# Cross attention with half-size products for keys and queries, and a first projection on rows without the root

## The chip, the core and the metric

The kernel runs on one core of a Trainium2 chip. TensorE multiplies, VectorE (DVE) and ScalarE (ACT) add, scale, copy and take functions, GpSimd (POOL) helps a little, and SyncE (SP) issues the weight transfers. The metric is the time of one execution on the device in microseconds; of several runs the median counts.

## The reference, cut to what matters

Two transformer blocks follow each other over 256 tokens of width 1024, in float32. The first block has two layers. Each layer is a mixer (a gated recurrence with forgetting attention in layer 0, dilated and sliding-window attention in layer 1), then cross attention to 256 memory rows, then an MLP with squared relu. The second block is a hybrid mixer and a mixture of 16 experts. The change touches the first projection of layer 0 and the cross attention of both layers:

```python
def rmsnorm(x, g):
    y = x * rsqrt(mean(x * x, axis=-1) + EPS)
    return y * g
z = rmsnorm(h, ab_norm) @ w_in        # u, gate, q, k, v, f_logit are its parts
...
mem_n = rmsnorm(mem, g_mem)
q = (h @ w_q).reshape(b, s, 4, 256)   # h is rmsnorm(h, xa_norm) here
k, v = split(mem_n @ w_kv, 2)
sc = einsum("bqhd,bkhd->bhqk", q, k) * 256 ** -0.5
o = einsum("bhqk,bkhd->bqhd", softmax(sc), v)
out = o.reshape(b, s, 1024) @ w_o
```

## The kernel before, in words

Activations lie transposed: 128 partitions hold one chunk of the width, the free dimension holds the 256 tokens, and a tile such as `xT` or `hT` has eight chunks. Dense weights come in units of 1024 rows by 512 columns (2 MB) through a ring of six slots. SP issues unit after unit in a fixed order; a unit for a slot waits until the products that read the slot's former unit are done (`unit_read`, L1436). The order of work on each engine is written out by hand; engines meet at semaphores. `filled` and `freed` count uses of the eight PSUM banks; `full` waits for a finished bank, `copied` for one that has been read out.

`columns` multiplies one unit: for each of four groups of 128 output columns eight products accumulate (weights stationary 128x128, rows moving, 256 columns), 32 in all. The profile shows each such float32 product as two MATMUL records with two weight loads. `mm` (L482) is the helper that most of them share.

At the start SP loads x and waits for it before it issues unit 0. TensorE runs 24 fillers on a constant tile (L825). ScalarE squares x, TensorE sums the squares over the partitions with a tile of ones (`norm("ab")`, eight products), ScalarE takes the root, VectorE the reciprocal (L1919), and scales the rows by root and gain into `hT` (L1927). Then TensorE makes `ab_f` (eight columns of forget logits), `ab_u` (unit 0), `ab_gate` (unit 1), the gates' small products and the units for q, k and v. ScalarE copies `ab_u` into the padded tile `up`, on which VectorE runs the convolution. Ahead of that VectorE computes a short chain of decay constants (`log1p` on `sp_t`, up to L2045).

Cross attention of a layer (`cross`) is two key units (`columns` on the memory rows `raw`, banks 5 and 6 for the first), the product of the norm's sum between them, two value units, two query units, the attention of four heads of 256, and the output projection. The value units (L885) already use seven products of half-size blocks in place of eight (a Winograd form of Strassen's scheme): VectorE forms four sums of weight blocks (`vw`, 128x1024 each) and four of memory-row blocks (`vh`, 128x512 each) in `prepare_values`, and combines the products in `collect_values` (L2158 and on). There the rows are stationary and 256 weight columns move. The up-projection of the MLP (`up_columns`, L941) uses the same scheme the other way round: weight blocks are stationary, 128 tokens move, 56 products for a unit. ScalarE copies keys and queries out of PSUM, the queries with the factor 1/16. Scores of heads 0 and 1 come between the halves of the second query unit. VectorE first normalizes `hT` for the queries (`norm`), then prepares the value sums.

Further on, from some 1180 us, the expert weights (96 units of 2 MB) stream in.

## Time and profile before

| | us |
|---|---|
| median of 3 runs (1681.64 to 1685.13) | 1684.67 |
| the profiled execution's own time | 1685.47 |
| its span, first to last instruction | 1683.7 |
| TensorE busy | 1502.4 (89%) |
| VectorE busy | 693.7 (41%) |
| ScalarE busy | 288.8 (17%) |
| mean granted TensorE clock, as a share | 0.944 |

The span is what the rows cover. A busy TensorE is the sum of stretches in which a matmul record was open. In rows of a timeline the second number is the length of the group, and a bracket gives the engine's idle time before it and what released it. In rows of groups the mean is that of one record.

### The profile page before, as it was taken

The numbers are of one execution on the slowest core, as the hardware profiler recorded it, in microseconds if no ns is written. First come the engines' busy times: TensorE is split into PE (matmuls) and PEld (weight loads), VectorE is DVE, ScalarE is ACT, GpSimd is POOL, SyncE is SP. The second block draws the span as 40 slices with busy tenths as digits, with TensorE's granted clock in tenths as the row PEclk, the third lists the DMA queues.
The fourth block names the chain that finished last, engine by engine and source line by source line (L and its number), as shares of the span: only waits on it lengthen the run. The fifth ranks groups of instructions, "written<-read, shape, count | busy, mean of one in ns | idle before, by whom it ended". The sixth has DMA issues, their size and how long they took to land.

```text
span 1683.7 us, 22615 instructions
## 1 busy us (share of the span) xinstructions
PE 1502.4 (89%) x9686; PEld 1157.3 (69%) x9686; DVE 693.7 (41%) x1448; ACT 288.8 (17%) x722; POOL 30.2 (2%) x52
## 2 busy tenths in 40 slices
PE   9999999999999999999999999989988566665666
PEld 7878889998877788899988887768863221221211
DVE  4635218788524441288876746823230000000000
ACT  1332012310112411222101322221020000000000
POOL 0000000000010000000000111000000000000000
PEclk9999999999999999999999999988999897888777
DMA  9525415866433053257763003232889999999997
GB/s 382 199 86 194 156 51 213 306 267 227 176 118 144 20 193 144 80 223 305 270 229 138 1 11 115 101 101 101 349 334 427 428 428 428 428 429 428 429 429 330
DMA packets 45107, 396.44 MB, mean 235 GB/s; under 512 B 16208, under 2 KB 18640, under 8 KB 20176
## 3 DMA queue, kind: packets, MB, share of 16 engines
q1 hardware_dynamic: 44304, 393.51, 58.7%
q8 instruction: 77, 1.26, 0.3%
q0 software_dynamic: 272, 1.05, 0.2%
q10 hardware_dynamic: 432, 0.44, 0.1%
q14 instruction: 22, 0.18, 0.0%
HBM read 392.36 MB, written 2.63 MB: 235 GB/s over the span
## 4 chain that ended last, share of the span: by engine, by line
PE 75%; DMA 22%; DVE 1%; SPq 1%; ACT 1%; issue 1%; DVEq 0%; ACTq 0%
PE pb L482 41%; DMA ring<-in_w_experts 21%; PE pb L977 11%; PE pb L941 10%; PE pb L580 7%; PE pb L885 3%; DMA inverses_turned<-arena 1%; PE pb L649 1%; SPq L1440 0%; PE pb L825 0%; ACT arena L1503 0%; PE pb L707 0%; SPq L1397 0%; ACT hT L1503 0%; PE pb L988 0%
## 5 line engine op out<-in xcount | busy, mean ns | idle before, releaser
L482 PE MATMUL pb<-hT,ring 128*128 128x256 f32 x1216 | 278.0, 387 | 0.0
L482 PEld LDWEIGHTS pb<-hT,ring 128*128 128x128 f32 x1216 | 232.5, 193 | 39.3 <-issue 7.8
L482 PE MATMUL pb<-ring,hT 128*32 128x512 f32 (+2 forms) x896 | 145.8, 656 | 62.9 <-DMA ring<-in_w_experts 61.7
L482 PEld LDWEIGHTS pb<-ring,hT 128*32 128x32 f32 (+1 forms) x896 | 45.1, 131 | 153.1 <-DMA ring<-in_w_experts 82.3
L1503 ACT ACTIVATE arena<-pb 128x512 f32<-128x512 f32 (+4 forms) x141 | 65.2, 477 | 366.8 <-PE pb L482 272.1
L2703 DVE SCALAR_TENSOR_TENSOR side<-side,pb 128x256 f32<-128x256 f32 x16 | 6.7, 421 | 272.2 <-ACT side L1503 272.2
L580 PE MATMUL pb<-arena,ring 128*128 128x256 f32 x512 | 118.6, 383 | 0.0
L580 PEld LDWEIGHTS pb<-arena,ring 128*128 128x128 f32 x512 | 95.3, 191 | 14.7 <-issue 2.9
L1503 ACT ACTIVATE side<-pb 128x256 f32<-128x256 f32 (+2 forms) x44 | 18.5, 421 | 442.5 <-PE pb L482 424.7
L482 PE MATMUL pb<-arena 128*64 128x128 f32 (+4 forms) x464 | 71.2, 338 | 4.6 <-DVE sml L1978 2.7
L482 PE MATMUL pb<-arena,hT 128*32 128x512 f32 x216 | 38.8, 845 | 35.5 <-DMA arena<-in_w_experts 23.2
L482 PEld LDWEIGHTS pb<-arena 128*64 128x64 f32 (+2 forms) x464 | 50.6, 173 | 23.3 <-issue 18.8
L2177 DVE CUSTOM_DVE_ANT_0 ring<-ring,arena,cols 128x1024 f32<-128x1024 f32 x48 | 59.2, 1281 | 0.0
L977 PE MATMUL pb<-ring,arena 128*128 128x256 f32 x256 | 58.2, 379 | 0.0
L977 PE MATMUL pb<-arena,hT 128*128 128x256 f32 x256 | 57.9, 379 | 0.0
L977 PE MATMUL pb<-ring,hT 128*128 128x256 f32 x256 | 57.9, 379 | 0.0
L482 PE MATMUL pb<-arena,side 128*32 128x256 f32 (+1 forms) x464 | 43.3, 474 | 15.6 <-DMA arena<-in_w_experts 8.9
L482 PE MATMUL pb<-root_pairs,ring 128*128 128x256 f32 (+1 forms) x288 | 54.3, 338 | 0.7 <-DMA ring<-inverses 0.7
L941 PE MATMUL pb<-hT,ring 128*128 128x128 f32 x448 | 54.6, 275 | 0.0
L2715 DVE TENSOR_TENSOR arena<-pb,rstd 128x256 f32<-128x256 f32 x16 | 6.8, 425 | 113.6 <-PE pb L482 113.6
L977 PEld LDWEIGHTS pb<-arena,hT 128*128 128x128 f32 x256 | 48.6, 190 | 6.6
L977 PEld LDWEIGHTS pb<-ring,hT 128*128 128x128 f32 x256 | 48.6, 190 | 6.6
(376 smaller groups left out, 2187.2 us busy)
## 6 DMA issues: line engine op xcount, KB each, us to landing
ring<-in_w_dense SPq DMA_DIRECT2D x86, 2048.0 KB, 8.0
ring<-in_w_experts SPq DMA_DIRECT2D x63, 2048.0 KB, 41.0
arena<-in_w_experts SPq DMA_DIRECT2D x22, 2048.0 KB, 40.7
arena<-in_w_experts SPq DMA_DIRECT2D x10, 1024.0 KB, 36.8
cons<-in_w_experts SPq DMA_DIRECT2D x10, 1024.0 KB, 40.1
ring<-in_w_dense SPq DMA_DIRECT2D x2, 1536.0 KB, 7.1
ring<-in_w_experts SPq DMA_DIRECT2D x4, 512.0 KB, 36.1
cons<-in_cons SPq DMA_DIRECT2D x1, 1808.0 KB, 17.9
```

Of the source, the lines that this page charges most:

```text
L482: return nc.tensor.matmul(o, l, r, start=st, stop=sp)
L580: last = nc.tensor.matmul(proj["banks"][c // 2][:, (c % 2) * S:(c % 2 + 1) * S], w[:, k, (c % 4) * P:(c % 4 + 1) * P], yT[:, k, :], start= ...
L649: last = nc.tensor.transpose(ps[:, c:c + P], pr2[:, n % 4, qb, kb * P:(kb + 1) * P], ident)
L885: last = nc.tensor.matmul(pv[j[0]][:, FEAT[j[1]]], rows_[l](k), cols_[r](k), start=k == 0 and n < 4, stop=k == 3, skip_group_check=True)
L941: last = nc.tensor.matmul(ps[b][:, o:o + P], lhs[x][:, k, f * P:(f + 1) * P], rhs[x][:, k, :], start=x in "156" and f == 0 and k == 0, sto ...
L977: last = nc.tensor.matmul(pq[j[0]][:, FEAT[j[1]]], rows_[l](k), cols_[r](k), start=g == 0 and k == 0 and n < 4, stop=g == 3 and k == 3, sk ...
L1503: return nc.scalar.activation(o, i, f, **kw)
L2177: ins = V.tensor_tensor_reduce(out=w, in0=w, in1=c_row, scale=1.0, scalar=col("b_ada", 4 * i + f), op0=ALU.mult, op1=ALU.add, accum_out=mo ...
L2703: V.scalar_tensor_tensor(tg[:, e % 2, :], tg[:, e % 2, :], 1.0, ps[:, 0:S], ALU.add, ALU.mult).then_inc(eg_ready, 1)
L2715: V.tensor_tensor(yq[:, e % 2, :], ps[:, 0:S], rs[:, :], ALU.mult).then_inc(free, 1)
```

## The change

At the start the wait for x on SP goes, and unit 0 comes in four quarters, each with a semaphore. VectorE scales the rows of x by the gain only (`raw_x`), sums the squares in pairs as other norms do, and TensorE multiplies unit 0 with these rows right behind 20 fillers (`first_unit`), one chunk of the width after the other, with one product of the squares' sum after the third chunk. VectorE multiplies `ab_u` by the reciprocal root when it copies it into `up`; ScalarE does not copy it any more. `ab_f` comes behind `ab_u`.

In cross attention the second key unit and both query units go through `cross_columns`: seven products of half-size blocks, each eight matmuls of 128 moving tokens with stationary weight blocks, in the order 1, 5, 6, 7, 4, 2, 3. The weight sums go through the three buffers `vw` (the fourth is formed in place in the slot), the row sums through `vh`: those of the memory rows serve the keys and then the values, those of `hT` both query units. ScalarE copies the first product (`first_block`) and the last block (`last_block`); VectorE adds the other three blocks (`block_22`, `block_21`, `block_12`). The factor 1/16 moves into the gain of the norm (`g16`). Value units keep their products; their weight sums are now single steps (`weight_sum`) between others. The scaling of the memory rows for layer 1 moves behind the norm's pair sums.

```diff
-        SUMMED = ("mem", "xa0", "mlp0", "cd", "xa1", "mlp1", "final")
+        SUMMED = ("ab", "mem", "xa0", "mlp0", "cd", "xa1", "mlp1", "final")
...
+            def first_unit():
+                u = at[0]
+                at[0] += 1
+                w = slot_ap(u)
+                ps = [fill(f"ab_u{b}") for b in range(2)]
+                for k in range(DC):
+                    if k % 2 == 0:
+                        if k < 6:
+                            pe.wait_ge(first_part[k // 2], 16)
+                        else:
+                            pe.wait_ge(loaded[slot_of[u]], 16)
+                    pe.wait_ge(raw_x_ready, k + 1)
+                    for b in range(2):
+                        for j in range(2):
+                            last = nc.tensor.matmul(ps[b][:, j * S:(j + 1) * S], w[:, k, (2 * b + j) * P:(2 * b + j + 1) * P], raw_x[:, k, :],
+                                                    start=k == 0 and j == 0, stop=k == DC - 1, skip_group_check=True)
+                        if k == DC - 1:
+                            mark(last, f"ab_u{b}", u=u if b else None)
+                    if k == 2:
+                        norm_of_sum("ab")
...
-            for i in range(24):
+            for i in range(20):
...
-            norm("ab")
+            first_unit()
...
-            columns("ab_u", hT)
...
+            def cross_columns(layer, which, banks, middle=None):
...
+                place = {"1": (0, 0), "2": (0, 0), "4": (0, 1), "5": (1, 0), "3": (1, 0), "6": (2, 0), "7": (2, 1)}
+                lhs = {"1": w[:, HALF[0], FEAT[0]], "5": vw[0], "6": vw[1], "7": w[:, HALF[0], FEAT[1]], "4": vw[2],
+                       "2": w[:, HALF[1], FEAT[0]], "3": w[:, HALF[1], FEAT[1]]}
+                rhs = {"1": m[0][:, :, TOK[0]], "5": vh[0], "6": vh[1], "7": vh[2], "4": m[1][:, :, TOK[1]],
+                       "2": m[1][:, :, TOK[0]], "3": vh[3]}
+                for x in "1567423":
+                    b, side_ = place[x]
+                    name = f"x{which}{layer}_{b}"
+                    if x in "156":
+                        ps[b] = fill(name, banks[b])
+                    if x in "5674":
+                        pe.wait_ge(vw_ready, weight_sums(layer, which, "5674".index(x) + 1))
+                    if which != "q1" and x in "5673":
+                        pe.wait_ge(vh_ready, 8 * layer + 4 * (which == "q0") + "5673".index(x) + 1)
+                    if x == "4":
+                        pe.wait_ge(q1_copied, n + 1)
+                    if x == "3":
+                        pe.wait_ge(out_ready, blocks_out_of(layer, which, 1))
+                    for f in range(2):
+                        for k in range(4):
+                            if which == "q0" and x == "1" and f == 0:
+                                pe.wait_ge(h_ready, (8, 32)[layer] + k + 1)
+                            o = side_ * S + f * P
+                            last = nc.tensor.matmul(ps[b][:, o:o + P], lhs[x][:, k, f * P:(f + 1) * P], rhs[x][:, k, :],
+                                                    start=x in "156" and f == 0 and k == 0, stop=x not in "15" and k == 3,
+                                                    skip_group_check=True)
+                    mark(last, name, True, u if x == "3" else None)
+                    product_done["cross", layer, which, x] = (banks[b], marks[banks[b]])
+                    if x == "6" and middle is not None:
+                        middle()
...
-                columns(f"xk{layer}_1_", raw)
+                cross_columns(layer, "k", (4, 7, 5))
...
+                cross_columns(layer, "q0", (0, 1, 2))
...
+                cross_columns(layer, "q1", (3, 6, 7), first_scores)
...
-            sp.wait_ge(x_in, 16)
...
+                if u == 0:
+                    for i in range(4):
+                        part = slice(i * UNIT // 4, (i + 1) * UNIT // 4)
+                        sp.dma_start(t[:, at:at + UNIT][:, part], w[:, part]).then_inc(first_part[i] if i < 3 else loaded[slot_of[u]], 16)
+                elif u < len(units) - 1:
...
-            act.wait_ge(pads, 1)
-            for i in range(2):
-                copy(f"ab_u{i}", up[:, 2 * i:2 * i + 2, 3:3 + S], pairs)
...
+            def first_block(layer, which):
+                b, m = product_done["cross", layer, which, "1"]
+                act.wait_ge(filled[b], m)
+                fn(block_of(layer, which)[1], pairs(pb[:, b, :])[:, 0, :].rearrange("p (f t) -> p f t", f=2), ACT.Copy).then_inc(q1_copied, 1)
+            def last_block(layer, which):
+                b, _, use = fillings[f"x{which}{layer}_0"]
+                act.wait_ge(out_ready, blocks_out_of(layer, which, 2))
+                fn(block_of(layer, which)[0], pairs(pb[:, b, :])[:, 0, :].rearrange("p (f t) -> p f t", f=2), ACT.Copy).then_inc(freed[b], 1)
...
-                for j in range(2):
-                    copy(f"xk{layer}_1_{j}", kT[:, 4 + 2 * j:6 + 2 * j, :], pairs)
+                first_block(layer, "k")
+                last_block(layer, "k")
...
-                for i in range(3):
-                    copy_q(i)
-                attention(f"xa{layer}", None, lambda: copy_q(3))
+                first_block(layer, "q0")
+                last_block(layer, "q0")
+                first_block(layer, "q1")
+                attention(f"xa{layer}", None, lambda: last_block(layer, "q1"))
...
+            dve.wait_ge(x_in, 16)
+            for c in range(DC):
+                V.tensor_scalar(raw_x[:, c, :], xT[:, c, :], col("ab_norm", c), None, ALU.mult).then_inc(raw_x_ready, 1)
+            sum_pairs("ab")
+            V.tensor_scalar(g16, cols[:, COLS["xa_norm0"][0]:COLS["xa_norm0"][0] + 16], 1.0 / 16, None, ALU.mult).then_inc(g16_ready, 1)
...
+            for i in range(2):
+                ps, free = full(dve, f"ab_u{i}")
+                dve.wait_ge(pads, 1)
+                V.tensor_tensor(up[:, 2 * i:2 * i + 2, 3:3 + S], pairs(ps), by_rstd(2), ALU.mult).then_inc(free, 1)
...
-            dve.wait_ge(mn_ready, 8)
-            V.tensor_tensor(memT, memT, by_rstd(DC), ALU.mult).then_inc(mn_ready, 1)
...
+                dve.wait_ge(g16_ready, 1)
+                dve.wait_ge(mn_ready, 9 * layer + 8)
+                for x in (1, 2, 3):
+                    row_sum(layer, "k", x)
+                    weight_sum(layer, "k", x)
                 sum_pairs(f"xa{layer}")
-                norm(f"xa{layer}", lambda c: col(f"xa_norm{layer}", c))
-                prepare_values(layer, 0)
-                prepare_values(layer, 1)
+                weight_sum(layer, "k", 4)
+                row_sum(layer, "k", 4)
+                if layer == 0:
+                    V.tensor_tensor(memT, memT, by_rstd(DC), ALU.mult).then_inc(mn_ready, 1)
+                weight_sum(layer, "v0", 1)
+                weight_sum(layer, "v0", 2)
+                block_22(layer, "k")
+                block_21(layer, "k")
+                weight_sum(layer, "v0", 4)
+                weight_sum(layer, "v0", 3)
+                block_12(layer, "k")
+                norm(f"xa{layer}", lambda c: g16[:, 8 * layer + c:8 * layer + c + 1])
+                for x in (1, 2, 4, 3):
+                    weight_sum(layer, "v1", x)
                 collect_values(layer, 0)
+                dve.wait_ge(h_ready, (16, 40)[layer])
+                for x in (1, 2):
+                    row_sum(layer, "q0", x)
+                    weight_sum(layer, "q0", x)
+                weight_sum(layer, "q0", 3)
+                weight_sum(layer, "q0", 4)
+                row_sum(layer, "q0", 3)
+                row_sum(layer, "q0", 4)
                 collect_values(layer, 1)
-                attention(f"xa{layer}")
+                weight_sum(layer, "q1", 1)
+                weight_sum(layer, "q1", 2)
+                block_22(layer, "q0")
+                weight_sum(layer, "q1", 3)
+                block_21(layer, "q0")
+                weight_sum(layer, "q1", 4)
+                block_12(layer, "q0")
+                def last_queries(h):
+                    if h == 0:
+                        block_22(layer, "q1")
+                        block_21(layer, "q1")
+                        block_12(layer, "q1")
+                attention(f"xa{layer}", last_queries)
...
-                m = [view(t, 0, 4, S) for t in (lru_w_, rtp)]
+                if n == 1:
+                    dve.wait_ge(loaded[slot_of[u]], 16 * nth[u])
...
+                    ins = V.tensor_tensor(vw[0], w12, w11, ALU.subtract)
+                elif n == 2:
+                    ins = V.tensor_tensor(vw[1], w22, vw[0], ALU.subtract)
+                elif n == 3:
+                    ins = V.tensor_tensor(w12, w22, w12, ALU.subtract)
+                else:
+                    ins = V.tensor_tensor(vw[2], vw[1], w21, ALU.subtract)
+                ins.then_inc(vw_ready, 1)
...
+            def product_of(b, side_):
+                return pb[:, b, FEAT[side_]].rearrange("p (f t) -> p f t", f=2)
+            def block_22(layer, which):
+                c11, c12, c21, c22 = block_of(layer, which)
+                dve.wait_ge(q1_copied, 3 * layer + THREE.index(which) + 1)
+                b = after_product(layer, which, "7")
+                link(V.tensor_tensor(c12, c12, product_of(b, 0), ALU.add))
+                V.tensor_tensor(c21, c12, product_of(b, 1), ALU.add).then_inc(freed[b], 1)
+                copied(dve, f"x{which}{layer}_2")
+                b = after_product(layer, which, "5")
+                V.tensor_tensor(c22, c21, product_of(b, 0), ALU.add).then_inc(out_ready, 1)
+            def block_21(layer, which):
+                dve.wait_ge(out_ready, blocks_out_of(layer, which, 1))
+                after_product(layer, which, "2")
+                b = after_product(layer, which, "4")
+                c21 = block_of(layer, which)[2]
+                V.tensor_tensor(c21, c21, product_of(b, 1), ALU.subtract).then_inc(out_ready, 1)
+            def block_12(layer, which):
+                b = after_product(layer, which, "3")
+                c12 = block_of(layer, which)[1]
+                V.tensor_tensor(c12, c12, product_of(b, 0), ALU.add).then_inc(freed[b], 1)
```

## Rows read from the trace of the kernel before

**Rows 1.** The page's chain that ended last, shares by engine.

```profile
PE 75%; DMA 22%; DVE 1%; SPq 1%; ACT 1%; issue 1%; DVEq 0%; ACTq 0%
```

**Rows 2.** Stretches: us, busy time by engine, clock, DMA share, GB/s.

```profile
1170.00:1180.00 10.00, 10.00 (x54) 7.93 (x53) 4.83 (x8) 0.00 (x0) 0.00 (x0) 1.00 0.01 2
1180.00:1190.00 10.00, 10.00 (x49) 8.79 (x48) 3.44 (x5) 0.00 (x0) 0.00 (x0) 1.00 0.87 339
1300.00:1400.00 100.00, 60.07 (x534) 21.22 (x529) 5.08 (x12) 5.73 (x17) 0.00 (x0) 0.88 1.01 429
```

**Rows 3.** What the DMA-issuing queue waited for: total us, times, longest.

```profile
SPq L1436 <- PE pb L482: 841.5, 106, 95.7
```

**Rows 4.** Timeline of the start: start us, us, engine, line, what, [idle, releaser].

```profile
1.05 7.37 PE L825 MATMUL pb<-more 128*128 128x128 f32 x48 [1.05 <-DVE more L2027]
...
6.38 2.56 ACT L1503 ACTIVATE arena<-xT 128x256 f32<-128x256 f32 x8 [2.54 <-DMA xT<-in_xT]
6.74 0.17 DVE L2029 TENSOR_SCALAR sml<-cols 128x4 f32<-128x4 f32 x1 [5.74 <-DMA cols<-in_cols]
...
8.27 3.62 PE L482 MATMUL pb<-arena,cons 128*128 128x256 f32 x16
...
12.49 1.75 DVE L1919 RECIPROCAL rstd<-root 128x256 f32<-128x256 f32 x1 [5.16 <-ACT root L1503]
...
14.28 3.26 DVE L1927 SCALAR_TENSOR_TENSOR hT<-xT,cols,rstd 128x256 f32<-128x256 f32 x8
...
14.91 5.30 PE L482 MATMUL pb<-hT,small_w 128*8 128x256 f32 x16 [3.03 <-DVE hT L1927]
...
20.14 27.89 PE L482 MATMUL pb<-hT,ring 128*128 128x256 f32 x128
...
20.92 0.47 DVE L2045 TENSOR_SCALAR arena<-pb,cols 8x256 f32<-8x256 f32 x1
...
54.95 1.14 DVE L2072 TENSOR_SCALAR side<-side,sml 128x256 f32<-128x256 f32 x4
```

**Rows 5.** A stretch of the start, columns as in rows 2.

```profile
15.00:17.00 2.00, 2.00 (x6) 0.60 (x6) 2.00 (x6) 0.00 (x0) 0.00 (x0) 0.50 1.05 451
```

**Rows 6.** DMA issues until 60 us: KB each, us to landing.

```profile
xT<-in_xT SPq DMA_DIRECT2D x1, 1024.0 KB, 5.6
...
cols<-in_cols ACTq DMA_DIRECT2D x1, 140.0 KB, 5.5
```

**Rows 7.** Timeline of TensorE in cross attention and MLP of layer 0.

```profile
148.42 1.89 PE L482 MATMUL pb<-lru_w,ring 128*128 128x256 f32 x8
...
162.24 1.89 PE L885 MATMUL pb<-ring,lru_w 128*128 128x256 f32 x8
...
272.33 1.95 PE L941 MATMUL pb<-hT,ring 128*128 128x128 f32 x16
...
284.84 1.95 PE L941 MATMUL pb<-hT,ring 128*128 128x128 f32 x16
```

**Rows 8.** Timeline of VectorE in cross attention of layer 0.

```profile
138.79 2.29 DVE L2098 TENSOR_TENSOR side<-side,rstd 128x2048 f32<-128x2048 f32 x1
140.99 2.14 DVE L1951 TENSOR_TENSOR arena<-arena 128x512 f32<-128x512 f32 x3
...
154.15 1.22 DVE L2130 TENSOR_TENSOR arena<-ring 128x1024 f32<-128x1024 f32 x1
155.28 0.69 DVE L2132 TENSOR_TENSOR arena<-lru_w,root_pairs 128x512 f32<-128x512 f32 x1
...
174.62 0.42 DVE L2158 TENSOR_TENSOR arena<-arena,pb 128x256 f32<-128x256 f32 x1 [1.12 <-PE pb L885]
```

**Rows 9.** Timeline of TensorE at two waits of cross attention.

```profile
217.49 0.60 PE L707 MATMUL pb<-cons,arena 128*128 128x128 f32 x4
218.70 1.53 PE L482 MATMUL pb<-arena 128*128 128x256 f32 x6 [0.61 <-ACT arena L1503]
...
616.29 1.97 PE L885 MATMUL pb<-ring,lru_w 128*128 128x256 f32 x8 [0.78 <-ACT arena L1503]
```

More of the change, by code:

```diff
@@ L865, in cross @@
                     value_unit[layer, i] = u
-                    n_ = 2 * layer + i
                     pv = {}
@@ new lines, in after_product, with weight_sum @@
+            def after_product(layer, which, x):
+                if which[0] == "v":
+                    b, done = product_done["value", layer, int(which[1]), (0, 4, 6, 1, 2, 3, 5)["1432567".index(x)]]
+                else:
+                    b, done = product_done["cross", layer, which, x]
+                dve.wait_ge(filled[b], done)
+                return b
+            def weight_sum(layer, which, n):
+                u = value_unit[layer, int(which[1])] if which[0] == "v" else cross_unit[layer, which]
+                order = (1, 2, 4, 3) if which[0] == "v" else (1, 2, 3, 4)
```

92 lines of the change are left out of this document (49 added, 43 removed).

## The prediction

> **What bounds the kernel now.** I read four views. First the chain that ended last: TensorE holds 75% of the span, the DMA engines 22% [rows 1]. Second, where the one gives way to the other. From 1170 to 1180 us TensorE is busy all the time and the DMA engines 1% of it; in the next ten microseconds they are busy 87%, and in the expert stage (1300 to 1400) 101% at 429 GB/s, while TensorE waits for weights [rows 2]. So the kernel has a part bound by TensorE, up to about 1180 us, and a part bound by the stream of expert weights behind it. Third, what starts that stream: the queue that issues the weights spent 841.5 us waiting for products at L482 alone, 106 times, to free a ring slot [rows 3]. The stream is of fixed length and hangs on TensorE's progress, so a microsecond cut from TensorE before 1180 us should come off the end too. Fourth, the places of the change: the first 48 us, and cross attention in both layers. In the reader's rows TensorE idles 3.03 us near the start [rows 4] and 0.61 and 0.78 us in cross attention [rows 9]; otherwise it goes from one product to the next. What is removed from TensorE there is a gain, if VectorE and ScalarE keep up.
>
> **The start, step by step.** Now the order on TensorE is: 24 fillers (1.05 to 8.4), eight products of the square sums (from 8.27), root, reciprocal (12.49, 1.75), eight scalings (14.28, 3.26), then `ab_f` at 14.91, `ab_u` at 20.14 [rows 4]. `ab_u` and `ab_gate` together are 128 records in 27.89 us; a product of 256 columns is two records, so one product costs 0.436 us and a unit of 32 costs 13.9 us; `ab_gate` begins at 20.14 + 13.95 = 34.1 us. The stretch from 15 to 17 us, right behind the idle time, shows 0.50, the lower of the two levels, 1.2 GHz, which is why `ab_f` takes 5.2 us where eight products at 0.436 would be 3.5 [rows 4, 5].
>
> After the change TensorE multiplies unit 0 by rows that carry only the gain; the root moves to VectorE's copy of the result. When can it begin? Twenty fillers instead of 24 save four at the later, faster pace: a pass of 128 columns is 0.112 us (12.51 / 112) [rows 7], two each, 0.9 us, so they end near 7.5. x is there at 6.38 and the columns of constants at 6.74 [rows 4]; four scalings of this shape take 1.14 us [rows 4], so raw row 0 is ready at about 7.1 and all eight at 9.1. The first quarter of the weights, 512 KB, sits right behind x in the queue: at the stream's 429 GB/s [rows 2] it needs 1.2 us, so it lands near 7.8 and each following one 1.2 us later, while TensorE wants one per 3.5 us. Start: 7.8. The unit takes 13.9, the one product of the summed squares 0.4 inside it, `ab_f` 3.5 at the full clock, since no idle stretch is left ahead of it. `ab_gate` begins at 25.6 instead of 34.1: **8.5 us less**.
>
> What must stay hidden for that. The square sum: squares done 6.38 + 2.56 = 8.94; three pair sums 2.14 (as the same three at 140.99 [rows 8]) and a last one of 0.42 end at 11.9; TensorE asks for it after the third row chunk, 7.8 + 12 x 0.436 = 13.0. Then root, reciprocal and eight scalings, 0.5 + 1.75 + 3.26, end at 19.2 and `ab_f` asks at 22.1. VectorE then does the small chain of the decay constants, 3.4 us in all (now between the end of the scalings at 17.5 and the next operation at 20.92 [rows 4]), to 22.6, and the two copies with the reciprocal root, 0.7 us each as any 512-wide operation [rows 8], to 24.0. `ab_gate` needs their banks at 25.6. Smallest slack here 1.1 us. Without that cover each microsecond late is one lost. The convolution behind it starts earlier than now, so nothing in the recurrence is later against TensorE. On SP the wait for x goes; all later issues wait for products and move with them. The fillers' end is the other side: were x there sooner, 7.5 is the floor; that is 0.3 more.
>
> **Cross attention, step by step.** The second key unit runs from 148.42 (its first product) to 162.24 (first value product): 13.82 us for 32 products of 256 columns [rows 7]. The new form is 7 x 8 = 56 products of 128 columns. The up-projection of the MLP already has that form (L941, seven products per unit, stationary weights, the same shapes): one unit from 272.33 to 284.84, 12.51 us [rows 7]. So a unit saves 1.31 us, and three units in each of two layers **7.9 us**.
>
> At this place the Trainium skill has a rule that speaks against the change (TensorE: Matmul & The Clock Gate, Back-to-back issue gap): with a weight load ahead of each product it measures about 81 ns per product at 128 columns against 56 alone. By it the half-size products would lose 45%: 12.51 x 81 / 56 = 18.1 us per unit, 4.3 more than now, and the kernel would be 26 us slower in these units by that estimate. The rows have the very pairing, at 112 ns per record of 128 columns where half of a 256-column record is 108; so the loads cost 4%, not 45%, and I go by the rows.
>
> Now the sums. VectorE gets per unit four weight sums of 1.22 us, for keys and first queries four row sums of 0.69 (those of the keys only move ahead, the values used them already), and five block sums of 0.42; ScalarE's four 512-wide copies per pair of units become two 256-wide ones per unit of some 0.3 us (2.56 / 8) [rows 4]. Per layer new on VectorE: 12 x 1.22 + 4 x 0.69 + 15 x 0.42 = 23.7 us in some 80 us of TensorE's time. I followed the order in layer 0, in times of the old trace. Keys: three row and three weight sums, 5.7 us at most, now stand before the pair sums of the norm, and the scaling of the memory rows, 2.29 us, moves behind them. From 138.8 that makes 138.8 + 5.7 + 2.1 + 0.4 = 147.0 [rows 8]; TensorE asks for the sum one product ahead of 148.42, at 148.0: slack 1.0, the smallest. The fourth sums end at 148.9, wanted at 155.5. The seventh product is done at 155.6 and the block sums 1.4 us later; the last product asks at 159.1. Values: their first sum is ready at 153, wanted at 164. Queries: the row buffers are free when the second value unit has used them, 178.2, 179.9, 183.4, 185.1; the sums end at 186.0; the first query unit starts at 185.1 and wants them one by one from 186.9 to 195.8. The second wants its sums from 199.4, has them from 190 to 197.8. Its block sums stand behind two row maxima and one scaling, are done at 210.3 in this frame, wanted at 211.8. So all of it lies beside TensorE, each with a microsecond or more left.
>
> Two waits change. At the end of the queries TensorE resumes 1.21 us after the turn's start (217.49 to 218.70), because a 512-wide copy stood ahead [rows 9]. Afterwards the last thing is one block sum: it starts 0.3 us behind the last product's end as at 174.62 [rows 8], takes 0.42, so about 0.8: 0.4 less, twice, **0.8 us**. In layer 1 the value unit waited 0.78 us for a bank that ScalarE had yet to copy (616.29) [rows 9]; the new keys use other banks, and that wait goes, with its restart **0.9 us**. Bounds: nothing to 1.7 together.
>
> **Sum.** 8.5 + 7.9 + 0.8 + 0.9 = 18.1 us. The profiled execution took 1685.5 us around a span of 1683.7; that gives 1667.4. The median of the runs shown is 1684.67, 0.8 below the profiled one, which gives 1666.6. I say 1667.0.
>
> **Rivals.** (a) The start brings less, because x and the gains come later once the queue is full. x needed 5.6 us and the small constants, on another queue, 5.5 [rows 6], with little beside them; now 2 MB of unit 0 and then more stand behind x at once. If the quarters share the engines with both, x comes up to 2 MB / 429 GB/s = 4.9 us later, the gain is 3.6 instead of 8.5: 1672. For it: the two queues already ran side by side. Against it: unit 0 is issued after x on the same queue. The Trainium skill says that descriptors of one queue start in order on each DMA engine but that transfers issued by different engines interleave (DMA: Bandwidth & Descriptors, Two DMAs through the same engine are not ordered, Issuing engines are not separate DMA queues); by that x keeps its place and only the constants can slip. No row of before settles it. If TensorE waits so long that the clock falls again, some 2 us more go.
>
> (b) The gain is hidden: TensorE is shorter, but the expert stream ends when it did. This needs a stream that does not follow TensorE; DMA share 0.01 just before it and the waits for products [rows 2, 3] speak against. 1685.
>
> (c) Slower: VectorE becomes the bound of the cross units. Place: each product waits for a sum that waits for the buffer of the product before. If none of it were covered, a unit would pay 4 x 1.22 + 3 x 0.42 and its row sums, about 7 us, six units 42: 1667 + 42 = 1709. It decides from 3 us uncovered per unit (18.1 / 6). For it: only three weight buffers and long chains of waits; against it: the slacks above, and the up-projection, which runs the same scheme with no idle time ahead of its products between 272 and 285.
>
> (d) The change doesn't do what it says, for instance the 56 products run slower from these tiles: half the unit gain, 1671, in the range of the first.
>
> **How the numbers follow.** Forecast 0.80 (own range 1664.5 to 1670, from the floor of 7.5, the two waits at their bounds, and one microsecond each way for where low-clock stretches fall); (a) and (d) 0.13; (b) 0.03; (c) 0.04. The 80% range takes in (a): 1664 to 1673. No change that a measurement could tell is within 0.2%, 3.4 us: faster 0.93, same 0.03, slower 0.04.
>
> **What would show it.** In the trace of after: first products of the ring's weights at about 7.8 us and the clock at 1.00 from then on; `ab_gate` at 25.6; seven groups of 16 records at 1.79 us in each cross unit; no idle of TensorE over 0.5 us from the keys to the scores; the stream's onset 18 us earlier, at 1163. A late x, an idle stretch ahead of "3" products, or an onset that stays at 1181 would prove it wrong.

## The result, and the profile after

The changed kernel took 1660.54 us, median of 4 runs (1657.76 to 1667.34), beside 1684.90 of the kernel before: ratio 0.9865, 95% interval 0.9831 to 0.9899. The forecast was 1667.0 with a range of 1664 to 1673; the kernel is faster than the range allows. The profiled execution took 1657.76 us around a span of 1656.0, 27.7 less than before, where the sum promised 18.1.

A few words are used throughout. A landmark is the start of one and the same product in two traces. The onset is the issue of the first transfer of expert weights on SP's queue. The work of a change is what it takes from TensorE's time between landmarks that have no stretch at the lower clock between them. Only at the start does it count a stretch at the lower clock with it: the 1.7 us that `ab_f` lost behind the idle time, which the change removes.

The page's chain of waits, by engine, which answers to [rows 1], and behind it the weight queue's largest group of waits, against [rows 3] (the new form of the cross units, at L926, has another 80.7 us of them).

```profile
PE 74%; DMA 23%; DVE 1%; SPq 1%; ACT 1%; issue 0%; DVEq 0%; ACTq 0%
```

```profile
SPq L1513 <- PE pb L498: 725.8, 99, 90.8
```

Stretches of the changed kernel, columns as in [rows 2]. The full-rate stream of expert weights, which began behind 1180 us before, now begins at 1150.70; in the expert stage the stream runs at the same rate (428 GB/s, 429 before).

```profile
1140.00:1150.00 10.00, 10.00 (x55) 7.92 (x54) 4.67 (x7) 0.00 (x0) 0.00 (x0) 1.00 0.01 2
1150.00:1160.00 10.00, 10.00 (x48) 8.81 (x47) 3.44 (x5) 0.00 (x0) 0.00 (x0) 1.00 0.91 357
1300.00:1400.00 100.00, 61.63 (x520) 21.18 (x512) 5.07 (x12) 5.70 (x17) 0.00 (x0) 0.84 1.01 428
```

The timeline of the start, against [rows 4]; behind it the stretch of [rows 5] and the two DMA issues of [rows 6].

```profile
8.39 2.19 DVE L2115 TENSOR_SCALAR arena<-xT,cols 128x256 f32<-128x256 f32 x8 [7.39 <-DMA cols<-in_cols]
8.89 5.42 PE L854 MATMUL pb<-arena,ring 128*128 128x256 f32 x24 [1.48 <-DVE arena L2115]
12.67 0.42 DVE L2036 TENSOR_TENSOR arena<-arena 128x256 f32<-128x256 f32 x1
14.15 0.59 PE L498 MATMUL pb<-arena,cons 128*128 128x256 f32 x2
17.14 3.26 DVE L2011 SCALAR_TENSOR_TENSOR hT<-xT,cols,rstd 128x256 f32<-128x256 f32 x8
23.30 3.62 PE L498 MATMUL pb<-hT,small_w 128*8 128x256 f32 x16
26.85 14.08 PE L498 MATMUL pb<-hT,ring 128*128 128x256 f32 x64
40.77 3.62 PE L498 MATMUL pb<-side,lru_w 128*128 128x256 f32 x16
```

```profile
15.00:17.00 2.00, 2.00 (x11) 1.76 (x10) 1.65 (x1) 1.90 (x4) 0.00 (x0) 1.00 0.88 371
```

```profile
xT<-in_xT SPq DMA_DIRECT2D x1, 1024.0 KB, 5.8
cols<-in_cols ACTq DMA_DIRECT2D x1, 140.0 KB, 7.1
```

The first of the four quarters of the weights, and below it the recurrence's small products in the kernel before:

```profile
ring<-in_w_dense SPq DMA_DIRECT2D x1, 512.0 KB, 7.0
```

```profile
47.87 3.62 PE L482 MATMUL pb<-side,lru_w 128*128 128x256 f32 x16
```

`ab_f` now runs at 1.00, in 3.62 us instead of 5.30, and `ab_gate` stands at 26.85. The first product came at 8.89 because VectorE had to wait for the columns of constants, which now need 7.1 us from issue to landing where they needed 5.5 [rows 6]. The first quarter, issued at 1.23 us, was there at about 8.2. The recurrence's small products (L498, `side` x `lru_w`) were at 47.87 before and are at 40.77: the start gives 7.1 us.

TensorE in the second key unit of layer 0, against [rows 7], and at the end of the queries, against [rows 9]:

```profile
141.32 1.95 PE L926 MATMUL pb<-lru_w,ring 128*128 128x128 f32 x16
143.10 3.74 PE L926 MATMUL pb<-arena 128*128 128x128 f32 x32
146.68 1.95 PE L926 MATMUL pb<-arena,ring 128*128 128x128 f32 x16
148.46 1.95 PE L926 MATMUL pb<-root_pairs,arena 128*128 128x128 f32 x16
150.25 1.95 PE L926 MATMUL pb<-root_pairs,ring 128*128 128x128 f32 x16
152.04 1.95 PE L926 MATMUL pb<-more,ring 128*128 128x128 f32 x16
153.82 1.89 PE L959 MATMUL pb<-ring,lru_w 128*128 128x256 f32 x8
...
207.23 0.63 PE L723 MATMUL pb<-cons,arena 128*128 128x128 f32 x4 [0.60 <-DVE arena L2316]
```

The unit takes 153.82 - 141.32 = 12.50 us instead of 13.82, with no idle time between its groups. VectorE beside it, against [rows 8]:

```profile
136.90 2.13 DVE L2035 TENSOR_TENSOR arena<-arena 128x512 f32<-128x512 f32 x3
139.06 0.42 DVE L2036 TENSOR_TENSOR arena<-arena 128x256 f32<-128x256 f32 x1
152.29 0.42 DVE L2310 TENSOR_TENSOR arena<-arena,pb 128x256 f32<-128x256 f32 x1 [2.23 <-PE pb L926]
```

The summed squares were ready at 139.5 for a product at 140.89: 1.4 us of slack where 1.0 was forecast. VectorE is busy 744.0 us instead of 693.7, beside TensorE.

**How much is work, and how much is something else.** I took the start of the same product in both traces. From the first key unit of layer 0 to the first up-projection behind it TensorE needs 120.09 us (127.08 to 247.17) instead of 123.91 (134.18 to 258.09), 3.8 less. In layer 1:

```profile
573.94 1.89 PE L498 MATMUL pb<-lru_w,ring 128*128 128x256 f32 x8
694.03 1.89 PE L498 MATMUL pb<-lru_w,ring 128*128 128x256 f32 x8
```

120.09 again, where the kernel before needs 124.76 (these two rows of its trace): 4.7 less.

```profile
587.29 1.89 PE L482 MATMUL pb<-lru_w,ring 128*128 128x256 f32 x8
712.05 1.89 PE L482 MATMUL pb<-lru_w,ring 128*128 128x256 f32 x8
```

So the work that the change takes away is 7.1 + 3.8 + 4.7 = 15.6 us, less than the 18.1 forecast. The two spans differ by 12.1 us more than that. That rest lies where the change touched nothing; first the kernel before, then the one after, in the same two parts of the program (the mixer of layer 1; from the first product of the hybrid mixer, at 913.08 and 895.07, to the onset, at 1180.98 and 1150.70). The last but two column is the granted clock.

```profile
536.00:546.00 10.00, 8.65 (x52) 6.40 (x52) 6.29 (x35) 6.21 (x25) 0.00 (x0) 0.66 0.12 52
913.00:1181.00 268.00, 260.53 (x1795) 212.33 (x1794) 144.76 (x360) 69.83 (x154) 21.70 (x39) 0.94 0.23 75
```

```profile
525.00:535.00 10.00, 8.57 (x64) 6.05 (x64) 6.79 (x37) 6.65 (x26) 0.00 (x0) 1.00 0.16 65
895.00:1151.00 256.00, 247.50 (x1796) 202.04 (x1794) 144.84 (x360) 69.88 (x154) 21.72 (x39) 0.99 0.24 78
```

Before, TensorE ran at 0.50 (1.2 GHz) for some 7 us of the mixer and in several stretches behind 932 us. After, none of this in the mixer and one stretch near 1100. The same matmuls take 268 us in one trace and 256 in the other.

### The profile page after: what moved, and what is told of

It is laid out like the page before. It is cut to its first block, busy times and chain, and to the rows that moved or that the text cites. A ratio compares the mean times of both kernels' runs of the same rounds, so it can differ in the third digit from the quotient of the medians.

```text
span 1656.0 us, 23299 instructions
## 1 busy us (share of the span) xinstructions
PE 1475.0 (89%) x9952; PEld 1144.1 (69%) x9952; DVE 744.0 (45%) x1525; ACT 285.2 (17%) x720; POOL 30.2 (2%) x52
## 4 chain that ended last, share of the span: by engine, by line
PE 74%; DMA 23%; DVE 1%; SPq 1%; ACT 1%; issue 0%; DVEq 0%; ACTq 0%
PE pb L498 34%; DMA ring<-in_w_experts 21%; PE pb L1051 12%; PE pb L1015 11%; PE pb L596 7%; PE pb L926 5%; PE pb L959 3%; PE pb L854 1%; DMA inverses_turned<-arena 1%; PE pb L665 1%; DMA cols<-in_cols 0%; PE pb L723 0%; SPq L1517 0%; ACT hT L1580 0%; SPq L1471 0%
## 5 line engine op out<-in xcount | busy, mean ns | idle before, releaser
L498 PE MATMUL pb<-ring,hT 128*32 128x512 f32 (+2 forms) x896 | 148.1, 675 | 65.4 <-DMA ring<-in_w_experts 64.1
L498 PE MATMUL pb<-hT,ring 128*128 128x256 f32 x896 | 202.7, 383 | 0.0
L498 PEld LDWEIGHTS pb<-hT,ring 128*128 128x128 f32 x896 | 168.2, 191 | 29.4 <-issue 7.6
L498 PEld LDWEIGHTS pb<-ring,hT 128*32 128x32 f32 (+1 forms) x896 | 43.5, 131 | 160.5 <-DMA ring<-in_w_experts 82.9
L498 PE MATMUL pb<-arena 128*64 128x128 f32 (+4 forms) x464 | 69.8, 331 | 3.5 <-DVE sml L2062 2.7
L498 PE MATMUL pb<-arena,hT 128*32 128x512 f32 x216 | 40.3, 877 | 35.8 <-DMA arena<-in_w_experts 23.1
L498 PEld LDWEIGHTS pb<-arena 128*64 128x64 f32 (+2 forms) x464 | 49.6, 168 | 21.7 <-issue 17.0
L498 PE MATMUL pb<-arena,side 128*32 128x256 f32 (+1 forms) x464 | 42.3, 464 | 15.0 <-DMA arena<-in_w_experts 9.3
L1051 PEld LDWEIGHTS pb<-ring,arena 128*128 128x128 f32 x256 | 48.3, 190 | 6.4
```

Of the source, the lines that this page charges most:

```text
L498: return nc.tensor.matmul(o, l, r, start=st, stop=sp)
L1051: last = nc.tensor.matmul(pq[j[0]][:, FEAT[j[1]]], rows_[l](k), cols_[r](k), start=g == 0 and k == 0 and n < 4, stop=g == 3 and k == 3, sk ...
```

## Experiments

In each, "mean" is that of the spans of its runs, set against the 57 such runs of the kernel before that were taken beside them (mean 1681.8 us, mean granted clock 0.946; they came in three groups on three chips, whose means are 1681.7, 1681.8 and 1681.6); the number behind ± is one standard error. "Lost" is the sum over windows of two microseconds of (1 - granted clock) x 2 us, from the hybrid mixer to the onset of the stream.

Fillers are those of the start. Dummies are the same kind of thing further on: products of a constant tile with itself, whose result nobody reads.

| kernel | mean of spans against before | mean clock | lost | stream's onset | profiled span |
|---|---|---|---|---|---|
| before | 0 | 0.946 | 17.1 | 1181.0 | 1683.7 |
| changed, first profile | -21.0 ± 1.4 (8 runs) | 0.951 | 3.4 | 1150.7 | 1656.0 |
| changed, again | (the same 8) | | 13.7 | 1160.2 | 1665.9 |
| start only | -8.4 ± 1.5 | 0.950 | 13.6 | 1170.3 | 1672.8 |
| cross only | -16.9 ± 2.1 | 0.951 | 13.7 | 1167.0 | 1669.4 |
| constants first | -19.2 ± 1.2 | 0.950 | 10.2 | 1157.2 | 1659.5 |
| before, 8 more fillers | +0.5 ± 0.7 | 0.947 | 15.4 | 1177.0 | 1685.1 |
| before, 16 more fillers | +1.0 ± 1.2 | 0.949 | 15.4 | 1179.6 | 1681.8 |
| before, dummies, first try | -4.7 ± 1.4 | 0.952 | 5.1 | 1173.3 | 1675.0 |
| changed, dummies, first try | -15.2 ± 1.3 | 0.949 | 12.0 | 1164.6 | 1670.2 |
| before, 10 dummies in mixer | -4.2 ± 0.8 | 0.950 | 10.2 | 1171 | 1674.1 |
| changed, 10 dummies in mixer | -22.4 ± 2.5 | 0.952 | 13.6 | 1158 | 1661.5 |
| changed, 16 more fillers | -21.8 ± 1.9 | 0.953 | 5.1 | 1155 | 1656.7 |
| changed, constants first, dummies | -25.4 ± 1.4 | 0.957 | 5.1 | 1150.5 | 1652.5 |

**1. The changed kernel once more.** No edit.

> The changed kernel once more, for more runs of both. Theory A (the change saves 15.6 us of TensorE's time, 7.1 at the start and 8.5 in cross attention, and the other 12 us between the two profiled executions are stretches at the lower clock that fall by chance): the mean difference over many runs comes down toward 16 us, the changed kernel's runs spread over some 10 us, and its trace has low-clock stretches at other places than the first trace. Theory B (the change removes low-clock stretches for good, since it moves all later work against something fixed): the difference stays at 23 to 26 us and the stretches at 530 to 545, 930 to 985 and 1040 us of the kernel before stay absent.

Runs of 1658.96 to 1667.74 us, ratio 0.9881 (0.9863 to 0.9899). The same program was profiled again. The product that stood at 573.94 now starts at 576.18 (a row of the timeline, then the two stretches):

```profile
576.18 1.89 PE L498 MATMUL pb<-lru_w,ring 128*128 128x256 f32 x8
```

```profile
525.00:535.00 10.00, 8.65 (x54) 6.46 (x52) 6.26 (x35) 6.29 (x25) 0.00 (x0) 0.66 0.14 57
897.00:1160.00 263.00, 257.08 (x1796) 210.26 (x1795) 144.70 (x360) 69.82 (x154) 21.73 (x39) 0.95 0.23 76
```

The low stretch of the mixer is back (2.2 us later at the keys), and from the hybrid mixer to the onset it loses 10.3 us more and takes 7.3 longer. Together 9.5 at the onset, 9.9 in the span. With this profile the kernel stands 17.8 us below before, near the 15.6 of work. So a third of the first profile's gain was the execution's luck with the clock. Neither theory holds as written: the mixer's stretch came back, against theory B, but the mean of the four new runs is 20.0 ± 1.8 below before, between the 16 of theory A and the 23 to 26 of theory B.

**2 and 3. One part alone.** The start's half of the diff (`first_unit`, 20 fillers, quarters, the copy with the root), or the half of cross attention (`cross_columns` and its sums), each on the kernel before.

> The kernel before with the edit of the start alone. Both theories: the first gate product starts 7.1 to 7.3 us earlier than before and cross attention keeps its length, so 7.1 us less by the work itself. Theory A: the mean of the runs is 7 us below the kernel before, give or take its spread. Theory B: more than 7 where the shift also drops a low-clock stretch, up to 7 + 9.

> The kernel before with the edit of cross attention alone; start as before. By the work itself 3.8 us in layer 0 and 4.7 in layer 1, 8.5 us in all. Theory A: 8.5 us less on the mean, and nothing moves ahead of 148 us. Theory B: more, since the later stages sit earlier by 4 to 8.5 us.

```profile
40.70 3.62 PE L485 MATMUL pb<-side,lru_w 128*128 128x256 f32 x16
```

```profile
47.74 3.62 PE L497 MATMUL pb<-side,lru_w 128*128 128x256 f32 x16
583.37 1.89 PE L497 MATMUL pb<-lru_w,ring 128*128 128x256 f32 x8
703.46 1.89 PE L497 MATMUL pb<-lru_w,ring 128*128 128x256 f32 x8
```

In the traces the parts add up to the full change within some 0.3 us: the start alone gives 7.2 us at the recurrence's product and 7.4 at both landmarks of layer 1 (579.90 and 704.66). The cross part alone gives 0.1 at the recurrence's product and 3.9 at the keys of layer 1, and the stretch from there takes 120.09 us, as in the full change. In the means they differ. The start alone brings 8.4, within its error of 7.2. The cross part brings 16.9 against 8.5 of work, four standard errors apart: more than theory A allows. The profile of cross only has the same losses as the changed kernel's second profile and stands at -14.3, so even it does not show the mean's whole -16.9.

**4. The constants ahead of x.**

```diff
+            sp.dma_start(cols[:, :], a["cols"]).then_inc(small_in, 16)
             sp.dma_start(xT, a["xT"].rearrange("(c p) t -> p c t", p=P)).then_inc(x_in, 16)
...
-            act.dma_start(cols[:, :], a["cols"]).then_inc(small_in, 16)
```

> The changed kernel with the small constants (140 KB) on the queue of x, ahead of x, in place of ScalarE's queue. Theory: the raw rows started at 8.39 us because the constants landed only 7.1 us after their issue, beside the unit quarters; ahead of x they land by 4 us, x lands some 0.4 later (6.9), the raw rows start at 6.9 and the unit's first product at 7.8 or 7.9 when the first quarter lands, 1.0 us earlier than in the changed kernel, and 1.0 us comes off the end. Rival: the first product waits for the quarter instead and starts at 8.9 again, no gain.

```profile
7.33 2.19 DVE L2115 TENSOR_SCALAR arena<-xT,cols 128x256 f32<-128x256 f32 x8 [6.33 <-DMA xT<-in_xT]
8.59 3.69 PE L854 MATMUL pb<-arena,ring 128*128 128x256 f32 x16 [1.44 <-DMA ring<-in_w_dense]
```

VectorE starts 1.06 us sooner, but now the first quarter of the weights holds TensorE. It lands at about 8.5 here, behind the constants and x, and at about 8.2 in the changed kernel. So 0.3 us is gained instead of the 1.0 expected, nearly as the rival had it, and the late constants were only the last of two things. In no run was the first quarter there by 7.8, so the floor of 7.5 for the start was not in reach.

**5 and 6. Only later.** 8 or 16 more fillers in the kernel before (`range(24)` becomes `range(32)`, `range(40)`).

> The kernel before with 8 more filler products at the start and nothing else, so all work is the same and stands 1.8 us later. Theory A (low-clock stretches fall by chance, whatever the kernel): 1.8 us slower on the mean, 1685 to 1686. Theory B (where the low clock falls depends on where the work stands in time, and the kernel before happens to stand badly): a time that does not follow the 1.8 us, by 3 us or more to the fast side, and a wider spread than the 6 us of the kernel before.

> The kernel before with 16 more filler products, the same work 3.6 us later. Theory A: 3.6 us slower, 1687. Theory B: it need not follow either; a time at or below 1684 speaks for B.

Eight fillers cost nothing: `ab_f`, behind the same 3.03 us of idle time, now ran at the full clock and gave back what they took, so all stood where it had from 47.8 us on. Sixteen put the recurrence's product at 52.44, 4.6 later, and the keys of layer 1 at 589.96, 2.7 later; the mean rose by 1.0 ± 1.2 and the mean clock by 0.002. A shift does not reach the end whole, and the low stretches change with it. Between the theories this decides little: experiment 5 shifted nothing behind 47.8 us, and in experiment 6 the mean rose less than the 3.6 of theory A, by two errors, while the median of 1685.1 is not at or below the 1684 of theory B.

**7 and 8. Dummy products ahead of idle time, first try.** In the kernel before and the changed one; 12 dummies in the mixer, 12 and 5 ahead of the waits for the inverses' DMAs (the cut of the diff shows the first of the two).

```diff
+            def keep_warm(b, n):
+                for _ in range(n):
+                    nc.tensor.matmul(pb[:, b, 0:P], ident, ident, start=True, stop=True)
...
                     between(2 * i, 0)
+                    if i == 0 and item[0] == "dil":
+                        keep_warm(3, 12)
                     turn(item)
...
+            keep_warm(3, 12)
             pe.wait_ge(tc_in, 64)
```

> The kernel before with idle filler products in three places where TensorE waits: 12 of 128 columns ahead of the first turn of the layer 1 mixer's attention (it idles 2.7 us there for VectorE), 12 ahead of the wait for the first loaded inverses (2.8 us) and 5 ahead of the second. They cost nothing where they fit in the wait. If low clock behind these waits is what moved the times beside the work, the stretch at 537 to 544 us disappears in every profile, worth 2.3 us (13.35 - 11.02), and the two after 1117 shorten, worth up to 4: 1678 to 1681. If the waits are not what lowers the clock, no change or up to 2 us slower.

> The changed kernel with the same idle fillers. If low clock behind the waits made the changed kernel's spread, it comes down to 1657 to 1661 with a spread under 6 us, and the difference to the run of the kernel before with the same fillers is the work alone, 15.6 us, give or take 2. If the difference stays at 20 or more, the rest is low clock elsewhere (the narrow products at 930, 975, 1040 and 1147 us).

I had put the mixer's dummies behind the 2.7 us wait instead of into it. They ran at the low clock and cost 5.1 us (first row, kernel before). The ones at the DMA waits worked there (second row; the kernel before has 0.79 from 1112 to 1160).

```profile
537.34 5.11 PE L474 MATMUL pb<-cons 128*128 128x128 f32 x24
```

```profile
1112.00:1160.00 48.00, 45.36 (x783) 40.54 (x781) 12.71 (x28) 14.72 (x25) 2.94 (x3) 1.00 0.38 112
```

The kernel before came out 4.7 ± 1.4 faster, at 1679.0, within the 1678 to 1681 expected, but not by the mechanism expected, since its low stretch in the mixer stayed and the keys of layer 1 came 3.0 us later (590.28). The changed kernel came out at -15.2 ± 1.3, that is slower than without. The two differ by 10.5 ± 1.9, where 15.6 ± 2 was expected. In the changed kernel the clock fell all the same, one stage later, behind 1.82 us for which the profile shows no releaser:

```profile
1110.88 3.15 PE L503 MATMUL pb<-hT,ring 128*128 128x256 f32 x7 [1.82 <-issue]
```

As a test of the clock in both kernels the pair is inconclusive, by my misplacement.

**9 and 10. Ten dummies inside the mixer's wait, nothing else.**

```diff
                 lead()
+                if items[0][0] == "dil":
+                    keep_warm(3, 10)
                 for i, item in enumerate(items):
```

> The kernel before with ten dummy products (128x128 on the constant tile, 20 records) in the one place where TensorE idles 2.7 us, in the mixer of layer 1, ahead of the scores of the second pair; the dummies of the two kernels named busy stood one stage too late there. Theory A (the clock falls to its lower level because TensorE was idle just before): the stretch at 0.50 near 537 to 544 us is gone, the dummies fit into the idle time (2.2 of 2.7 us), the span is 2 to 2.5 us shorter than that of the kernel before, the mean over the runs likewise, some 1681. Rival (the narrow products behind the wait are what lowers it): the stretch at 0.50 stays between 535 and 545, and nothing is gained.

> The changed kernel with the same ten dummies in the same place. Theory A: no stretch at 0.50 between 524 and 533 us, and TensorE is at the second key unit of layer 1 at 573.9 as in the first profile of the changed kernel, not at 576.1 as in its second. The difference of the means to the kernel before with dummies is then 15.6 us of work plus what the stretches behind 900 us do, 16 to 20. Rival (the gap beyond the work has nothing to do with the clock): the difference of the two means stays at 21.

The kernel before with them:

```profile
533.26 2.47 PE L474 MATMUL pb<-cons 128*128 128x128 f32 x20 [0.91 <-DVE arena L2409]
538.44 1.73 PE L487 MATMUL pb<-arena 128*64 128x128 f32 x20 [0.78 <-ACT arena L1510]
584.79 1.89 PE L487 MATMUL pb<-lru_w,ring 128*128 128x256 f32 x8
```

```profile
533.00:543.00 10.00, 8.84 (x70) 6.70 (x70) 8.00 (x45) 7.04 (x28) 0.00 (x0) 1.00 0.43 180
```

Without them, in the kernel before:

```profile
535.14 0.93 PE L482 MATMUL pb<-arena 64*128 64x128 f32 x8 [2.72 <-DVE sml L1978]
538.85 3.13 PE L482 MATMUL pb<-arena 128*64 128x128 f32 x20 [0.78 <-ACT arena L1503]
```

The low stretch is gone in both, the narrow products behind the wait take 1.73 us instead of 3.13, and the first key unit of layer 1 in the kernel before begins 2.5 us earlier; that of the changed kernel is at 573.96, as in its first profile. Theory A held and its rival fell: with the idle time filled, the narrow products alone did not bring the low clock. This does not hang on two profiles. Of the eleven without dummies inside this wait, with 2.7 us of idle time each, ten show the clock at 0.50 in the mixer; the three with dummies inside it (experiments 9, 10 and 12) show 1.00 throughout. The mean of the kernel before fell by 4.2 ± 0.8, more than the 2 to 2.5 of the wait. The difference of the two means is 18.1 ± 2.6 where it was 21.0 ± 1.4; the expected 16 to 20 holds it, but so nearly does the rival's 21.

**11. The changed kernel, later.** `range(20)` becomes `range(36)`.

> The changed kernel with 36 fillers at the start instead of 20, which moves all of it some 3.6 us later (16 x 2 records of 0.112 us, less what the fillers cover of the wait for the first weights) and alters nothing else. Theory A (the remainder hangs on how the low stretches fall, and the changed kernel draws lower or higher with its place in time): the mean moves by the shift or by a different amount, anywhere from -1 to +8 us, and the low stretches of the profile differ from both profiles of the changed kernel. Rival (a fixed gain beyond the work): the mean is 1662.5 + 2 to 3.6, that is 1664.5 to 1666, and the low stretches are those of its second profile, all as much later.

The recurrence's product is 2.0 us later (42.79), the keys of layer 1 1.6 us later than in its second profile, and the mean span did not rise: 1660.0 ± 1.9 beside 1660.8 ± 1.4. The low stretches were fewer than in that profile (5.1 lost against 13.7). The rival's 1664.5 to 1666 (these count the time around the span, 1661.9 was measured) is missed, by one to two errors. So a fixed gain beyond the work is unlikely, but not excluded.

**12. Everything that helped, together.** Experiment 4's edit and experiment 10's.

> The changed kernel with the constants ahead of x on SP's queue and the ten dummies in the mixer of layer 1: the version that the runs point to. Constants first gave 0.2 to 0.3 us in its profile, the dummies should give 2.2 where the stretch at 0.50 would else stand. Theory A: mean over the runs 1660 to 1662, against 1662.5 of the changed kernel. Rival: no difference to the changed kernel (1662.5 or more).

Mean 1658.1 us of 4 runs (1654.31 to 1660.24), ratio to before 0.9851 (0.9828 to 0.9875), and 4.4 ± 1.9 below the changed kernel. That is faster than the 1660 to 1662 expected. It is the fastest version here, by an interval that still overlaps that of the changed kernel.

**All runs together.** Each run has its mean granted clock beside its span. Within a kernel the longer runs are those of the lower clock: correlation -0.85 over the 8 runs of the changed kernel, -0.59 over the 57 of before, -0.98 and -0.93 for cross only and for the changed kernel with ten dummies. Pooled within the 13 programs (149 runs) the slope is 8.4 us per 0.01 of clock. The changed kernel's mean clock is 0.0049 above that of before; by the slope that is 4.1 us, and it leaves 21.0 - 4.1 = 16.9 us, against 15.6 of work. For start only it leaves 5.8 (work 7.2), for cross only 13.0 (work 8.5; twice its error away), for the combination of all 16.7. This is an estimate from a correlation between runs; no experiment set the clock.

## Why the prediction was wrong

**What bounds the kernel: right.** From the stream's onset to the end it is 502.7 us before, 505.3 after, and 502 to 508 in every kernel above. What TensorE gains ahead of it comes off the end; rival (b) is out. In all profiles the stream began between 1150 and 1181, as TensorE reached it.

**The start: direction right, term too large.** 7.1 instead of 8.5. Of the step "raw row 0 is ready at about 7.1" the gain factors, which are among the columns of constants, were the late part (rival (a) in small: x came 5.8 us after its issue, not 10): the constants on the other queue slipped by 1.6 us once unit 0 was issued right behind x. This agrees with both rules of the Trainium skill that the prediction weighed there (DMA: Bandwidth & Descriptors, Two DMAs through the same engine are not ordered, Issuing engines are not separate DMA queues): x kept its place, 5.8 us to landing where it was 5.6, and the constants slipped, 7.1 where it was 5.5. The first quarter of the weights came late too, at about 8.2, 0.4 later than the 7.8 that the full stream rate gave; the constants cost the other 0.7 of the 1.1 us. The rest of the chain came as worked out: the summed squares at 13.1 (11.9 forecast, with the rows 1.3 late), the scalings' end at 20.4 (19.2 forecast), `ab_f` in 3.6 us at 1.00.

**The seven products: right.** 12.50 us a unit against 12.51, six units 7.9 us. A record of 128 columns with its weight load costs 112 ns, against 108 for half of a 256-column record, so the rival by the Trainium skill's 81 to 56 ns (TensorE: Matmul & The Clock Gate, Back-to-back issue gap) did not happen with these float32 records; rivals (c) and (d) did not happen. No product waits for a sum inside a unit.

**The two turns: wrong, small.** 0.8 was forecast and about -0.4 came. TensorE now waits 0.60 us ahead of the turn for the last block sum (L2316), in both layers, where it waited 0.61 and 0.45 us behind the turn's start. From the end of the queries' products to the scores behind the turn it is 1.3 us in both layers, and it was 1.2 and 1.0. The forecast had "0.4 less, twice"; the chain of product, block sum and transposes costs what the 512-wide copy had. It also breaks the forecast "no idle of TensorE over 0.5 us". The bank wait of layer 1 did go, with the 0.9 forecast: before, the value unit of layer 1 stood 0.9 us later behind its keys than that of layer 0, and now both stand alike. The terms as measured, 7.1 + 7.9 - 0.4 + 0.9, make 15.5, the work of the landmarks but for 0.1.

**The step that failed: the range.** By its own terms the sum was too generous, 18.1 against 15.6, yet the kernel came out faster than it: 24.4 us between the medians. The two errors have opposite signs. What failed is "one microsecond each way for where low-clock stretches fall". The kernel before had 17.1 us lost at 0.50 behind 913 us and 3.4 in the mixer, and no row of this went into the forecast; one profile stood for its state. Two profiles of one and the same program, the changed one, differ by 9.9 us, and the clock's losses ahead of the onset by 13.7 (10.3 and 3.4). Between the first two profiles the mixer gives 2.4 us of its account of 3.4, the part up to the onset 12.3 of 13.7 (1180.98 - 913.08 against 1150.70 - 895.07), and the stage behind takes 2.6 back (505.3 against 502.7): the 12.1 us beyond the work. In the means it is some 4 of 5.4 us. With this account in it the range runs from 1670 (15.6 of work, nothing of the account closed) down to 1649 (all 20.5 us of it closed), and it holds every run of the changed kernel. (It is drawn after the fact, and the account can grow as well as shrink.) The cost rule of the Trainium skill (TensorE: Matmul & The Clock Gate, HAM oscillation — how this bites in real kernels) is that half of the time spent at the lower clock is lost; the mixer shows less than that, 2.2 to 2.5 us for 3.4 by this count. TensorE also waits inside that stretch, and its waits of 0.24, 0.33 and 0.78 us are as long in the first profile of the changed kernel, where the clock is 1.00.

**What stays open.** That the idle time in the mixer has a part in lowering the clock is shown (experiments 9, 10 and 12). That it is not enough is shown too: in the changed kernel's first profile it changed nothing. Why the changed programs, and each half alone, draw a higher mean clock than the one before is not: shifts of the kernel in time alter it (0.001 and 0.002 in experiments 5 and 6), but none made the kernel before 5 us faster. Cross only is faster in the mean than its work and its clock account for. The runs of changed kernels also scatter more (standard deviation 3.8 us, start only 3.6, cross only 5.0, against 2.3 before). It is no mark of the change itself, since the kernel before scatters as much with 16 more fillers (3.9) and with the first dummies (4.9); the reason was not looked for.

## What to carry to other kernels

Compare two traces by landmarks that have no low-clock stretch between them, and here the work that a change removes repeated within 0.3 us from trace to trace, where the total times scattered by ten. Before a forecast, add up the time at the lower clock in the trace of before, by stretch: it is an account that any change can open or close, so it belongs in the range, and a single profile of the kernel says little about it. And the place of dummy products decides: ten inside a wait of 2.7 us brought 2.5 us, and twelve one step behind it cost 5.

## What the runs showed of the hardware

The clock fell in the middle of busy time too: at 976 us in the kernel before TensorE was busy 8.00 of 8 us at 0.60.

```profile
976.00:984.00 8.00, 8.00 (x46) 6.71 (x43) 2.31 (x4) 1.45 (x3) 0.00 (x0) 0.60 0.00 0
```

```profile
974.42 4.08 PE L482 MATMUL pb<-rstd,cons 16*64 16x256 f32 x32
```

Ahead of it stood products that use 16 of the 128 rows and 64 of the columns. They are not enough to lower it: in the first profile of the changed kernel the same products stand in the same place, and the clock stays at 1.00.

```profile
954.72 3.67 PE L498 MATMUL pb<-rstd,cons 16*64 16x256 f32 x32
```

```profile
956.00:966.00 10.00, 10.00 (x81) 8.48 (x76) 3.73 (x8) 2.43 (x5) 0.00 (x0) 1.00 0.01 2
```

Whether they have a part in it was not tried. The same idle time did not always have the same effect either: behind 3.03 us of it `ab_f` ran at the lower level in the kernel before, at the full one when it came 1.6 us later (experiment 5), and at the lower one again when it came 4.6 us later (experiment 6); and in the changed kernel's first profile the mixer kept 1.00 through its 2.71 us of idle time.
